# Value products of a pair of heads two gate tiles later, in front of the next score products, in a fused encoder kernel

## What is computed

```python
q, k, v, hy_in, gates = jnp.split(hn @ w_in[l], splits, axis=-1)
a_out = neighbourhood_attention(q, k, v, na_rpb[l])     # 8 heads of 64: softmax(q k / 8 + bias) v
b_out = hyena_mixer(short_conv(hy_in), h_fwd, h_bwd, ...)
g = sigmoid(gates + gate_b)                             # 2 x 1024 columns
merged = g[:, :, 0] * (a_out @ w_up_na) + g[:, :, 1] * (b_out @ w_up_hy)
x = x + merged @ w_out
x = x + peer(rmsnorm(x), ...)                           # 128 + 128 tiles of expert weights
```

## Time and profile before

| | us |
|---|---|
| median of 3 runs | 1985.32 (1984.79 to 1986.59) |
| the profiled execution: its own time | 1987.37 |
| the profiled execution: span | 1985.5 |
| PE busy | 1976.9 |
| POOL busy | 1599.6 |
| DVE busy | 1250.7 |
| ACT busy | 1118.1 |

### The profile page before, as it was taken

One profiled execution on the slowest core, in us unless ns is written; L12 is line 12 of the kernel. 1 busy time (PEld: TensorE's weight loads), 2 busy tenths in 40 slices (PEclk: granted clock), 3 DMA queues, 4 the chain that ended last, 5 costly groups with the idle time before them and its releaser, 6 DMA issues.

```text
span 1985.5 us, 41409 instructions
## 1 busy us (share of the span) xinstructions
PE 1976.9 (100%) x11924; PEld 1716.7 (86%) x11924; DVE 1250.7 (63%) x2807; ACT 1118.1 (56%) x2453; POOL 1599.6 (81%) x1316
## 2 busy tenths in 40 slices
PE   9999999999999999999999999999999999999999
PEld 8999888888888888888889898888888888888887
DVE  6787589888886333333377865998888863333333
ACT  6565566665555555555575556666555555555554
POOL 7767978887778888888877678899877778888886
PEclk9999999999999999999999999999999999999999
DMA  9544645554454555555674446455554455555554
GB/s 269 181 140 148 211 158 183 189 171 161 161 163 163 196 190 193 194 194 190 198 233 161 138 158 210 161 188 185 167 168 159 159 169 195 194 191 191 195 195 148
DMA packets 103396, 358.41 MB, mean 181 GB/s; under 512 B 11744, under 2 KB 16802, under 8 KB 103076
## 3 DMA queue, kind: packets, MB, share of 16 engines
q1 hardware_dynamic: 102900, 355.41, 54.7%
q10 hardware_dynamic: 432, 2.18, 0.3%
HBM read 356.49 MB, written 1.05 MB: 180 GB/s over the span
## 4 chain that ended last, share of the span: by engine, by line
PE 60%; POOL 23%; issue 15%; DVE 1%; POOLq 1%; ACT 0%; DMA 0%; DVEq 0%; ACTq 0%
PE bank L1984 35%; POOL w_lo L444 22%; PE bank L1630 14%; PE bank L1632 7%; PE bank L1923 3%; DVE raw_lo L959 0%; POOLq L442 0%; POOLq L465 0%; DMA cols_sb<-cols 0%; DVE weighted_j L1508 0%; ACT raw_hi L556 0%; PE bank L1595 0%; ACT w_hi L507 0%; DVE onehot_j L1502 0%; PE bank L2010 0%
## 5 line engine op out<-in xcount | busy, mean ns | idle before, releaser
L444 POOL TENSOR_TENSOR w_lo<-ring,w_hi 128x512 fp32r<-128x512 f32 x1048 | 1398.4, 1350 | 295.9 <-ACT w_hi L507 295.1
L507 ACT ACTIVATE w_hi<-ring 128x512 fp32r<-128x512 f32 x1312 | 752.7, 621 | 184.9 <-PE bank L1619 89.8
L1630 PE MATMUL bank<-act_parts,w_hi 128*128 128x512 f32 x2048 | 719.0, 396 | 0.7 <-POOL w_lo L444 0.2
L1632 PE MATMUL bank<-act_parts,w_lo 128*128 128x256 f32 x2048 | 569.6, 278 | 0.0
L444 DVE TENSOR_TENSOR w_lo<-ring,w_hi 128x512 fp32r<-128x512 f32 x256 | 236.6, 924 | 450.1 <-ACT w_hi L507 449.9
L1630 PEld LDWEIGHTS bank<-act_parts,w_hi 128*128 128x128 f32 x2048 | 384.2, 188 | 91.5 <-issue 1.7
L1984 PE MATMUL bank<-w_hi,e_hi 128*128 128x512 f32 x1024 | 398.9, 390 | 0.2
L1984 PE MATMUL bank<-w_hi,e_lo 128*128 128x512 f32 x1024 | 398.4, 389 | 0.0
L1984 PE MATMUL bank<-w_lo,e_hi 128*128 128x512 f32 x1024 | 398.4, 389 | 0.0
L1632 PEld LDWEIGHTS bank<-act_parts,w_lo 128*128 128x128 f32 x2048 | 385.2, 188 | 0.0
L843 ACT ACTIVATE e_hi<-arena 128x256 fp32r (+1 forms) x256 | 106.8, 418 | 315.8 <-PE bank L1984 315.8
(11 more groups left out here) (253 smaller groups left out, 2365.0 us busy)
## 6 DMA issues: line engine op xcount, KB each, us to landing
ring<-stream SPq DMA_DIRECT2D x654, 512.0 KB, 3.3
arena<-rpb_in SPq DMA_DIRECT2D x8, 512.0 KB, 7.9
arena<-dft_in SPq DMA_DIRECT2D x4, 512.0 KB, 4.9
arena<-subkeys ACTq DMA_DIRECT2D x2, 1024.0 KB, 8.2
ring<-stream SPq DMA_DIRECT2D x4, 256.0 KB, 5.0
xT<-x_in SPq DMA_DIRECT2D x4, 256.0 KB, 5.3
arena<-w_in SPq DMA_DIRECT2D x2, 512.0 KB
arena<-decay_in SPq DMA_DIRECT2D x2, 512.0 KB
```

Source lines behind the costliest of these rows:

```text
L444: eng.tensor_tensor(w_lo[:, part_, :], ring[:, tile % RING, half * HT:(half + 1) * HT], w_hi[:, part_, :].bitcast(F32), ALU.subtract).then ...
L507: nc.scalar.activation(w_hi[:, 2 * (tile % AHEAD) + half, :], ring[:, tile % RING, half * HT:(half + 1) * HT], ACT.Copy).then_inc(hi_ready ...
L1630: T.matmul(out_[:, 0:2 * S], weights(w_hi, tile, k), both[:, :, k, :], start=(k == 0), stop=False, skip_group_check=True)
L1632: ins = T.matmul(out_[:, 0:S], weights(w_lo, tile, k), both[:, 0, k, :], start=False, stop=(k == KT - 1), skip_group_check=True)
```

## The change

The value products of pair p are formed two gate tiles later: not behind G(4p+3) but behind G(4p+5), directly in front of the score products of pair p+2 (for the pair 2 in front of the turn of z; the last pair stays where it was). As the turned probabilities of the next pair are then written before they are read, `probs_T` gets a second place. On VectorE `attention_parts(p)` goes from in front of a convolution to behind the two head scores of pair p+2, and `attention_parts(2)` to the end of the loop. No instruction is added or removed.

```diff
--- before.py
+++ after.py
@@ -190,7 +190,7 @@
         qk_tmp = part(93, 3, S)
         spread = part(97, 2, P)
         even_part = part(69, 2, HW)
-        probs_T = part(101, 2, TT, S)
+        probs_T = [part(101, 2, TT, S), part(119, 2, TT, S)]
         dft = part(105, 4, TT, S)
         decay = part(113, TT, HW)
         skip = part(74, HW)
@@ -739,7 +739,7 @@
                 for h in range(NH):
                     gate(2 * h)
                     act.wait_ge(pT_done.sem, pT_done.at(l, h + 1))
-                    nc.scalar.activation(probs_T[:, h % 2, :, :], bank[6][:, :].rearrange(
+                    nc.scalar.activation(probs_T[h // 2 % 2][:, h % 2, :, :], bank[6][:, :].rearrange(
                         "p (k q) -> p k q", k=TT), ACT.Copy).then_inc(pT_ready.sem, 1)
                     if h % 2 and h + 1 < NH:
                         head_exp(h + 1)
@@ -1196,8 +1196,6 @@
                 tiles = [4, 8, 5, 9, 6, 10, 7, 11]
                 normalise_probs(0)
                 for p in range(NH // 2):
-                    if p:
-                        attention_parts(p - 1)
                     if tiles:
                         conv(tiles.pop(0))
                     normalise_probs(2 * p + 1)
@@ -1206,12 +1204,15 @@
                     if p + 1 < NH // 2:
                         head_scores(2 * p + 2)
                         head_scores(2 * p + 3)
+                        if p:
+                            attention_parts(p - 1)
                         if tiles:
                             conv(tiles.pop(0))
                         if p == 2:
                             V.tensor_tensor(zT[:, :, :], u[:, 4:8, :], u[:, 8:12, :], ALU.mult
                                             ).then_inc(z_ready.sem, 1)
                         normalise_probs(2 * p + 2)
+                attention_parts(NH // 2 - 2)
 
                 def mixed_halves(ri):
 
@@ -1797,6 +1798,17 @@
                     T.matmul(bank[4 + 2 * ri + e][:, :], dft[:, ri, e, 0:P], z_tok[:, e, :], start=True, stop=True
                              ).then_inc(zf_done.sem, 1)
 
+                def attend(p):
+
+                    if p:
+                        pe.wait_ge(attn_ready.sem, attn_ready.at(l, p))
+                    for kt in range(TT):
+                        for j in range(2):
+                            g = 2 * p + j
+                            ins = T.matmul(attn_ps[p][j * HD:(j + 1) * HD, :], v_tok[:, kt, g * HD:(g + 1) * HD],
+                                           probs_T[p % 2][:, j, kt, :], start=(kt == 0), stop=(kt == TT - 1))
+                    ins.then_inc(pv_done.sem, 1)
+
                 for h in range(NH):
                     project(T_GATE + 2 * h, 20 + 2 * h)
                     pe.wait_ge(probs_ready.sem, probs_ready.at(l, h + 1))
@@ -1814,19 +1826,13 @@
                     project(T_GATE + 2 * h + 1, 20 + 2 * h + 1)
                     pe.wait_ge(pT_ready.sem, pT_ready.at(l, h + 1))
                     if h % 2 == 0:
+                        if h:
+                            attend(h // 2 - 1)
                         if h + 2 < NH:
                             head_pair(h // 2 + 1)
                         else:
                             turn_mixed()
-                        continue
-                    if h >= 2:
-                        pe.wait_ge(attn_ready.sem, attn_ready.at(l, h // 2))
-                    for kt in range(TT):
-                        for j in range(2):
-                            g = h - 1 + j
-                            ins = T.matmul(attn_ps[h // 2][j * HD:(j + 1) * HD, :], v_tok[:, kt, g * HD:(g + 1) * HD],
-                                           probs_T[:, j, kt, :], start=(kt == 0), stop=(kt == TT - 1))
-                    ins.then_inc(pv_done.sem, 1)
+                attend(NH // 2 - 1)
 
                 def up(n, wait=None):
```

## The result

The changed kernel is slower: 1.0046 times the time before, interval 1.0037 to 1.0056. Six executions each were taken; the medians are 1997.89 us (1993.06 to 1998.64) and 1986.01 us (1984.79 to 1988.51), and by the medians alone the ratio would be 1.0060. The forecast was 1990.8 us, or 1.0028, in a range up to 1993.4: right in its sign and too low. The profiled execution took 1998.64 us, its span is 1996.9 us, 11.4 more than before.

What follows compares the result with a forecast made beforehand. TensorE, with VectorE's chain right behind it, bounds the stage up to T(6). 1.54 + 1.16 = 2.7 us a layer, twice 5.4, 5.5 with held operations, on the median 1985.32: 1990.8 us; range 1987.0 to 1993.4.

Steps and rivals of the forecast that it cites:

- TensorE's work: TensorE in the stage: no matmul added, fewer passages between small and full tiles; 0.4 us a layer saved.
- the direct passage from value products to scores: TensorE going from 64 columns to 64 rows: between nothing and 0.2 us, taken as 0.1.
- T(2): TensorE's turn for head 2: GpSimd's earlier pair holds norm 2's last operation; 108.04, +1.07 us, after 2.4 us waiting.
- S2: Score products of pair 2, behind postponed value products: next gate tile +2.1 us, VectorE waits 1 us for scores.
- T(4): TensorE's turn for head 4: at 122.75 instead of 122.07, +0.7 us, with VectorE just in time.
- T(6): TensorE's turn for head 6: norm 6 ready at 138.43, turn at 138.48 instead of 136.94, +1.54 us.
- The end of the stage: Behind the last gate tiles: value products 2 add 1.16 us, so all that follows is 2.7 us late a layer.
- rival D: The clock falls to 1.2 GHz for one gate tile behind each wait at T(2): 1996.6 us; chance 0.04.
- the stages behind it only start later: Everything behind the attention stage: none waits for anything with its own clock, so it is only shifted.
- Rival A: Only the postponed products count, T(6) stays at 136.94: 1.16 us a layer, 1987.6 us; chance 0.25.
- Rival B: TensorE alone is the bound; waits and passages go, 0.9 us a layer, 1983.5 us; chance 0.04.
- The mechanism of C: More VectorE operations held by GpSimd, each 0.9 to 1.05 us a layer: 1992.8 us; chance 0.15, within the forecast's 0.64.

Runs made afterwards that it cites:

- its order alone: The kernel before with VectorE's new order and TensorE's old one; measured 0.9989.
- pair 0 alone: The changed kernel with only the value products of pair 0 postponed, those of the other pairs at their old places; measured 1.0026.
- the scores first: The changed kernel with the score products ahead of the value products of the same place; measured 1.0025.
- pair 2 alone: The changed kernel with only the value products of pair 2 postponed, those of the other pairs at their old places; measured 1.0008.
- early norms: The changed kernel with norms 2, 4 and 6 directly behind the scores of their pair; measured 0.9995, a second time 0.9981.
- norm 2 early: The changed kernel with norm 2 in front of convolution 5 and nothing else moved; measured 1.0047.
- the third execution of the change: The changed kernel with no edit, given a third time against the kernel before; measured 1.0043, 1998.90 against 1990.03 us.

## Why the prediction was wrong in its size and right in its path

1. *TensorE's work*: saved 0.35 us a layer, forecast 0.4. Right; the direct passage from value products to scores was no special case (1.01 us from the one to the other, 111.18 to 112.19, where a step of value products took 1.02 before).
2. *T(2)*: right in cause and time (12.66 against 12.70 behind S1, a wait of 2.28 against 2.4). GpSimd's earlier pair holds the second division. The prediction says that G4 ends 1.1 us sooner and moves its times by 1.19; measured are 1.20. That VectorE's new order isn't enough for it is shown by its order alone (56.31), and that postponing pair 0 alone brings it is shown by that run (12.66, where 11.6 was expected without the hold).
3. *S2*: G6 moved as said, and VectorE waited 1.10 us. But that wait is not "an added wait of 1 us on the very chain that bounds T(4)": with the scores first it turns into a wait for the exponentials, and T(4) stays where it was. The times of this step were right, the role was not; since T(4) came out bound by TensorE anyway, it left no error in the sum.
4. *T(4)* and 5. *T(6)*: 27.37 and 43.08, forecast 27.41 and 43.14, no stall and 0.90 us. Right.
6. *The end of the stage*: +2.73 us a layer, forecast 2.7. Right, and the 5.46 us of two layers are the forecast's 5.4 to 5.5.

The step that failed is the one that says what follows behind T(2) and behind the stage: rival D's size and chance, and "the stages behind it only start later", which put the change of the rests at nothing. D had a chance of 0.04, "if it went to 1.2 GHz for one gate tile behind each such wait", and a price of 2.9 us each. The clock fell behind the wait of 2.27 or 2.28 us in 6 of 12 stages of the table, behind that of 3.54 us in both, and behind no other; each fall lasted 3.4 us and, behind the shorter wait, cost 1.4 to 1.5 us. The prediction's price took it that a whole gate tile of 2.88 us would run at half the clock. The mean of the measured falls is 1.5 us on the whole kernel with two such waits. It should have had a chance near one half per wait, at half the price: 5.5 + 1.5 = 7.0 us, on 1985.32 about 1992.3. The three comparisons of this kernel give 1.0046, 1.0028 and 1.0043, on the mean 1.0039 or 7.8 us; their medians lie 11.9, 5.7 and 8.9 us above those of before. Which of the two levels follows a given wait these runs don't tell: nothing in the order or in the instructions differs between layers 0 and 1.

The other part is that the forecast took the rests as constant. They are not: rest 0 lies between 928.97 and 935.70 us, rest 1 between 841.38 and 845.31, with no order by kernel that these single traces show. The execution profiled after had a long one of both, 4.6 us above that of before. So the profiled execution shows 5.5 us of structure, 1.5 of clock and 4.6 of longer rests, less 0.3 at the start. For the whole first comparison (+11.9 us by the medians) this is taken over from one profile of six executions; that five of them came out long together, at 1997.0 to 1998.6, the runs don't explain, and what picks the distance in the rests stays open. A range for one comparison needed some 5 us more on the upper side.

Rival A (only the postponed products, T(6) unmoved) is refuted for the full change, T(6) is 1.5 us later. It is exactly what pair 2 alone does. Rival B (TensorE the only bound) is refuted for this kernel, but its price, 0.9 us a layer, is what the changed kernel shows with early norms: 56.30 to 55.42. The mechanism of C didn't show: up to 44 us behind S1 of layer 0, 18 operations of 128x256 without a PSUM operand take over 0.65 us, before and after. That operations which read PSUM aren't held was right, too: with norm 2 early, GpSimd's pair runs from 114.93 to 117.50, and VectorE's L1172 at 115.75 takes 0.68 us beside it, L1021 at 117.07 0.41 us. It agrees with the rule of the Trainium skill that the prediction had ("SBUF — State Buffer", Who interferes with whom). So the change can pay, once the even norms are taken out from behind the convolutions: 0.35 us a layer in the stage (55.77 to 55.42), which is less than the whole time can tell.

## What to carry to other kernels

Bringing one engine to a wait earlier gives nothing where the other side is the bound, and it can cost: here an earlier end of a gate tile moved GpSimd's pair onto the very operation that was waited for, and T(2) came 1.0 us later. Take the waits away first (what is waited for goes ahead of what isn't), and then shorten the engine that waits. And a wait on TensorE, here of 2.3 us, may cost more than its own length: add the price of a clock fall times a chance, and read several executions before giving a single number to it.

## What was not expected of the hardware

- The granted clock can fall to the 1.2 GHz level behind 2.27 us of idle TensorE, in 6 of 12 cases, for 3.4 us; waits of 0.91 us or less in the stage never did it. The lower clock doesn't begin at one place behind the wait: in these six cases between 0.2 us before the turn starts (107.89 against 108.11 in the third execution of the change, layer 0) and 1.3 us behind it.
- The same instructions at the same granted clock run in one of two distances, 2.77 or 2.83 us a tile in the expert part, and in 26 of 28 rests keep it for some 50 tiles. What picks it is open; it isn't the load of 1 MB before it.
- How small the lead is that decides who is held. The prediction had one case, L1166 at 103.62 with the pair at 103.66, 1.61 us. Over the traces of all fourteen executions, with no subtraction running already, each of the 25 operations of 128x256 without a PSUM operand behind whose start GpSimd's subtraction came by 0.001 to 0.046 us was held (1.44 to 1.62 us); none was where it came 0.055 us or more behind, as L1162 at 107.63 with the pair at 107.73, 0.41 us.
